# Causal mask added by VectorE inside the search for the row maximum, in place of a bf16 product on TensorE

## The chip, the cores and the metric

The kernel runs on one core of one Trainium2 chip. Its time is the device time of that core in microseconds (us). The kernel before takes 991.48 us, the median of 3 runs from 991.26 to 991.74. Below, TensorE is PE (its weight loads are PEld), VectorE is DVE, ScalarE is ACT, GpSimd is POOL and SyncE is SP.

## The reference, cut to what matters

One layer of a hybrid encoder over 512 tokens of width 1024. The change touches its two causal mixers. Forgetting attention ("fox") has 8 heads of width 64 and works on blocks of 128 queries:

```
logits = einsum('bhqd,bhkd->bhqk', qi, kf) + ci[..., :, None] - c[..., None, :]
logits = jnp.where(kpos[None, :] <= qpos[:, None], logits, -jnp.inf)
p = jax.nn.softmax(logits, axis=-1)
```

The mLSTM ("ml", 4 heads of width 128) needs the same of a matrix of decay logarithms, which is masked with a lower triangle, and of which every row's maximum is taken before the exponential:

```
Dlog = jnp.where(tri, Dlog, -jnp.inf)
m_t = jnp.maximum(inter_log, jnp.max(Dlog, axis=-1))
Dw = jnp.exp(Dlog - m_t[..., None])
```

The rest of the layer (projections, causal convolution, gates, cross-attention over 256 memory rows, an MLP of width 4096, norms) is not touched.

## The kernel before, in words

All large weights are streamed in units (`UNITS`): a unit is a slab of 512 weight columns. SP loads them in lots of 1 MB into `stage`, ACT copies a pair of slabs to a rounded part `w_hi`, and DVE subtracts that from the original to give the rest, `w_lo`. A product is then three matmuls, high by high, high by low and low by high, all at line 1062 in `half`. A "half" is four slabs deep, so twelve matmuls of 512 columns.

`make_steps` writes one list of steps, and every engine runs the steps that concern it in the order of that list, with semaphores between engines. Softmax work is laid between the halves. The 16 fox tasks t (4 pairs of heads by 4 query blocks, `PAIRS` by `NT`) stand two halves apart: `pair_scores` t on PE, `pair_exp` and `pair_norm` on DVE and ACT behind it, `pair_turn` four halves later and `pair_values` six halves later. Task t has 128, 256, 384 or 512 keys as t runs through 0, 1, 2, 3 of each pair. The 16 ml tasks follow, one half apart. While the first half of the fox tasks run, the same DVE and ACT queues also do the causal convolution (lines 622, 685, 814, 863).

Fox scores (line 1126): for each of the two heads of a pair, four matmuls add up in a PSUM bank, bank 2 for the one head and bank 3 for the other. Each has 64 rows of the array, one head on rows 0 to 63, the other on rows 64 to 127, and the two run side by side. Then comes the mask (line 1128): for each head a matmul of the bf16 identity `ident_b` with `hide_b`, a 128x128 bf16 tile that holds -1e30 above the diagonal, added to the last 128 columns of the bank. The ml scores (lines 1170 to 1172) do the same in one bank of 2 and 3.

DVE then finds the maximum of each row: for fox one `tensor_reduce` over both banks, negated (line 929), for ml one over one bank (line 951). ACT takes the exponential with that maximum as its bias (lines 705, 719). ml also has an instruction that multiplies and sums in one (`tensor_tensor_reduce`, line 960).

The tiles that live through the kernel are allocated one behind another. All activations lie behind them, at offsets from `a0`, which is the end of the former (`nc.sbuf_base`). Before the change `a0` is 95360 bytes, which is 745 times 128.

Of the kernel before, what the change touches and what calls it, by code (L numbers as in the profile page):

```python
# [6 lines left out]
F32R = mybir.dt.float32r  # L7
BF16 = mybir.dt.bfloat16
I32 = mybir.dt.int32
# [4 lines left out]
P = 128  # L14
# [27 lines left out]
X0 = N_ML  # L42
KB = 1024


# [216 lines left out]
def trunk(nc, x, mem, norm_mix, norm_xattn, norm_mem, norm_mlp, w_in, b_fox_f, b_mlstm_i, b_mlstm_f,  # L262
# [6 lines left out]
    with ExitStack() as ctx:  # L269
# [3 lines left out]
        def sb(name, shape, dt=F32):  # L273
            return ctx.enter_context(nc.sbuf_tensor(name, shape, dt))
# [5 lines left out]
        ident = sb("ident", [P, P])  # L280
        ident_b = sb("ident_b", [P, P], BF16)
        hide_b = sb("hide_b", [P, P], BF16)
        rows = FOX_HEADS + ML_HEADS
# [28 lines left out]

        a0 = nc.sbuf_base

# [192 lines left out]
        def _(pool):  # L507
            n = 0

            def fill(ins):  # L510
                nonlocal n
                ins.then_inc(s_const, 1)
                n += 1

            fill(pool.memset(ones[:], 1.0))
            fill(pool.memset(ident[:], 0.0))
            fill(pool.memset(ident_b[:], 0.0))
            fill(pool.memset(hide_b[:], 0.0))
            fill(pool.memset(upto[:], 1.0))
# [6 lines left out]
            pool.wait_ge(s_const, n)  # L526
            for m in (ident, ident_b):
                fill(pool.affine_select(out=m[:], in_=m[:], compare_op=ALU.not_equal, fill=1.0, base=0,
                                        pattern=[[-1, P]], channel_multiplier=1))

            fill(pool.affine_select(out=hide_b[:], in_=hide_b[:], compare_op=ALU.is_ge, fill=HIDE, base=0,
                                    pattern=[[-1, P]], channel_multiplier=1))

# [49 lines left out]
        def _(act):  # L583
# [87 lines left out]
            for step, n in steps:  # L671
# [27 lines left out]
                elif step == "pair_exp":  # L699
                    keys = P * (n % NT + 1)  # L700
                    act.wait_ge(s_fpeak, n + 1)
                    if n >= 2:
                        act.wait_ge(s_fturn, n - 1)
                    for d in range(2):
                        act.activation((prob, prob_b)[n % 2][:, d, 0:keys], bank[2 + d][:, 0:keys], ACT.Exp,
                                       bias=peak[:, d:d + 1],
                                       accum_out=pair_total[:, n % 2, d:d + 1]).then_inc(s_fexp, 1)
                elif step == "pair_turned":
# [55 lines left out]
        def _(dve):  # L764
# [113 lines left out]
            for step, n in steps:  # L878
# [48 lines left out]
                elif step == "pair_exp":  # L927
                    dve.wait_ge(s_fscore, n + 1)
                    dve.tensor_reduce(peak[:], two[1][:, :, 0:P * (n % NT + 1)], AX_X, ALU.max, negate=True)\
                       .then_inc(s_fpeak, 1)  # L930
                elif step == "pair_norm":
# [15 lines left out]
                elif step == "probs":  # L947
                    h, i, keys = task(n)
                    i2, row = n % 2, FOX_HEADS + task(n)[0]
                    dve.wait_ge(s_score, n + 1)  # L950
                    link(dve.tensor_reduce(ml_m[:, i2, 0:1], bank[2 + i2][:, 0:keys], AX_X, ALU.max))

# [59 lines left out]
        def _(pe):  # L1012
# [98 lines left out]
            def pair_scores(t):  # L1111
                p, i = t // NT, t % NT
                keys, tok = P * (i + 1), slice(P * i, P * i + P)
                cols = slice(decay_at(i), decay_at(i) + keys)
                if t == 0:
                    pe.wait_ge(s_dlow, NT + 1)
                if i == 0:
                    taken(pe, GROUP0[UNIT["fox_k"]] + p)
                if t >= 1:
                    pe.wait_ge(s_fexp, 2 * t)  # L1120
                for q in range(4):
                    for d in range(2):
                        r = slice(FOX_HD * d, FOX_HD * d + FOX_HD)
                        still = pick[r, 2 * p + d:2 * p + d + 1].to_broadcast([FOX_HD, P]) if q == 3 else (fq_hi, fq_hi, fq_lo)[q][r, p, tok]
                        moving = decay[r, cols] if q == 3 else (fk_hi, fk_lo, fk_hi)[q][r, p, 0:keys]
                        pe.matmul(bank[2 + d][:, 0:keys], still, moving, start=(q == 0), stop=False)  # L1126
                for d in range(2):
                    ins = pe.matmul(bank[2 + d][:, P * i:keys], ident_b[:], hide_b[:], start=False, stop=True)
                ins.then_inc(s_fscore, 1)
# [28 lines left out]
            def scores(t):  # L1158
                h, i, keys = task(t)
                s = bank[2 + t % 2]  # L1160
                cols = slice(decay_at(i), decay_at(i) + keys)
                if t == 0:
                    pe.wait_ge(s_silu, KT)
                    pe.wait_ge(s_fpt, N_FOX)
                    pe.wait_ge(s_fexp, 2 * N_FOX)
                else:
                    pe.wait_ge(s_prob, t)
                if t >= 2:
                    pe.wait_ge(s_exp, t - 1)
                pe.matmul(bank[5][:, 0:keys], ml_q[:, h, P * i:P * i + P], ml_k[:, h, 0:keys], start=True, stop=True)  # L1170
                pe.matmul(s[:, 0:keys], pick[0:64, FOX_HEADS + h:FOX_HEADS + h + 1].to_broadcast([64, P]), decay[0:64, cols], start=True, stop=False)
                pe.matmul(s[:, P * i:keys], ident_b[:], hide_b[:], start=False, stop=True).then_inc(s_score, 1)

# [104 lines left out]
N_SMALL = 6  # L1278
N_CONST = 21

# [24 lines left out]
```

## Time and profile before

| | |
|---|---|
| time, median of 3 runs | 991.48 us (991.26 to 991.74) |
| the profiled execution's own time | 991.38 us |
| its span, first to last instruction | 989.6 us |
| mean granted TensorE clock | 0.995 |
| PE busy | 958.0 us, 97% of the span |
| DVE busy | 478.6 us, 48% |
| ACT busy | 349.6 us, 35% |
| POOL busy | 13.7 us, 1% |

The span leaves out 1.78 us before the first and behind the last instruction. Durations of matmuls are from entry to modelled end, and matmuls are pipelined: two that follow each other begin 0.23 us apart though each is given 0.39 us. What PE spends on one is read from the distance of starts. The share of busy time of DVE and ACT is an average over stages; in a stage where they and PE wait for each other in turn, a lower share can still set the pace.

### The profile page before, as it was taken

The page shows a single profiled execution, that of the slowest core. Times are in us where ns is not written, and L with a number is a line of the kernel's source. Part 1 is how long each engine was busy: PE and PEld are TensorE (multiplying, and loading weights), DVE is VectorE, ACT ScalarE, POOL GpSimd, SP SyncE. Part 2 cuts the span into 40 slices and gives each one's busy share as a digit, 9 for nine tenths or more (in the row PEclk, how much of TensorE's full clock was granted, in tenths as well). Part 3 has the DMA queues.
Part 4 walks back from the last instruction along what each step waited for, and adds up shares of the span by engine and source line. Part 5 has one row for each costly group of instructions (what it writes and reads, how often), then busy time and mean ns, then how long its engine had stood idle before and what let it go on. Part 6 is the DMA issues. An engine that isn't in the chain of part 4 may idle for free.

```text
span 989.6 us, 11656 instructions
## 1 busy us (share of the span) xinstructions
PE 958.0 (97%) x4681; PEld 776.8 (78%) x4681; DVE 478.6 (48%) x873; ACT 349.6 (35%) x562; POOL 13.7 (1%) x37
## 2 busy tenths in 40 slices
PE   7999999999998999999999999999999999999996
PEld 6778777777776788889877668888888888888885
DVE  5622666433557654677234435643344434334536
ACT  4431555434324323235244422442144123213411
POOL 4000000000000000000000000000000000000000
PEclk9999999999999999999999999999999999999999
DMA  8212221122112162333422222222223332222212
GB/s 280 94 37 83 86 86 43 44 85 85 45 42 86 43 255 85 107 128 113 164 85 85 86 85 85 86 85 85 85 86 99 126 117 86 85 85 85 88 41 85
DMA packets 44205, 92.60 MB, mean 94 GB/s; under 512 B 1676, under 2 KB 1768, under 8 KB 44152
## 3 DMA queue, kind: packets, MB, share of 16 engines
q1 hardware_dynamic: 42584, 86.54, 26.2%
q0 software_dynamic: 1568, 5.32, 1.7%
q8 instruction: 37, 0.61, 0.2%
q14 instruction: 16, 0.13, 0.0%
HBM read 89.76 MB, written 2.10 MB: 93 GB/s over the span
## 4 chain that ended last, share of the span: by engine, by line
PE 86%; DVE 8%; ACT 3%; issue 1%; DMA 1%; SPq 0%; ACTq 0%; DVEq 0%
PE bank L1062 75%; DVE w_lo L794 3%; PE bank L1232 1%; DVE conv_acc L814 1%; PE bank L1075 1%; PE bank L1183 1%; PE bank L1126 1%; PE bank L1170 1%; ACT w_hi L585 1%; DMA stage<-in_w_in 1%; PE bank L1153 1%; PE bank L1197 1%; PE bank L1138 1%; PE bank L1210 1%; PE bank L1086 1%
## 5 line engine op out<-in xcount | busy, mean ns | idle before, releaser
L1062 PE MATMUL bank<-act_hi,w_hi 128*128 128x512 f32 (+2 forms) x624 | 246.2, 395 | 2.4 <-DVE act_lo L890 2.4
L1062 PE MATMUL bank<-act_hi,w_lo 128*128 128x512 f32 (+2 forms) x624 | 241.1, 386 | 0.0
L1062 PE MATMUL bank<-act_lo,w_hi 128*128 128x512 f32 (+2 forms) x624 | 240.9, 386 | 0.0
L794 DVE TENSOR_TENSOR w_lo<-stage,w_hi 128x1024 fp32r<-128x1024 f32 x156 | 183.9, 1220 | 112.6 <-ACT w_hi L585 112.4
L585 ACT ACTIVATE w_hi<-stage 128x1024 fp32r<-128x1024 f32 x156 | 156.4, 1051 | 187.1 <-PE bank L1062 179.8
L1062 PE MATMUL bank<-w_hi,act_hi 128*128 128x512 f32 x448 | 176.8, 395 | 5.1 <-DVE act_lo L890 3.5
L1062 PE MATMUL bank<-w_lo,act_hi 128*128 128x512 f32 x448 | 175.1, 391 | 0.0
L1062 PE MATMUL bank<-w_hi,act_lo 128*128 128x512 f32 x448 | 175.0, 391 | 0.0
L1062 PEld LDWEIGHTS bank<-act_hi,w_hi 128*128 128x128 f32 x624 | 117.8, 189 | 24.7 <-issue 2.6
L1062 PEld LDWEIGHTS bank<-act_hi,w_lo 128*128 128x128 f32 x624 | 117.7, 189 | 23.8
L1062 PEld LDWEIGHTS bank<-act_lo,w_hi 128*128 128x128 f32 x624 | 117.9, 189 | 22.0
L1062 PEld LDWEIGHTS bank<-w_hi,act_hi 128*128 128x128 f32 x448 | 84.4, 188 | 23.6 <-DVE act_lo L890 4.0
L1062 PEld LDWEIGHTS bank<-w_hi,act_lo 128*128 128x128 f32 x448 | 84.5, 189 | 17.7
L1062 PEld LDWEIGHTS bank<-w_lo,act_hi 128*128 128x128 f32 x448 | 84.6, 189 | 17.2 <-issue 0.2
L847 DVE TENSOR_TENSOR h_tok<-bank,h_tok 128x512 f32<-128x512 f32 x48 | 33.1, 689 | 92.5 <-PE bank L1062 91.8
L853 DVE TENSOR_TENSOR relu<-relu 128x512 f32<-128x512 f32 x32 | 22.1, 690 | 64.8 <-ACT relu L646 64.8
L646 ACT ACTIVATE relu<-bank 128x512 f32<-128x512 f32 x32 | 19.2, 599 | 77.9 <-PE bank L1062 77.9
L856 DVE TENSOR_TENSOR act_lo<-relu,act_hi 128x512 fp32r<-128x512 f32 x32 | 22.2, 693 | 22.4 <-ACT act_hi L585 22.4
L585 ACT ACTIVATE act_hi<-bank 128x512 fp32r<-128x512 f32 x32 | 17.7, 596 | 37.2 <-PE bank L1075 30.0
L585 ACT ACTIVATE act_hi<-relu 128x512 fp32r<-128x512 f32 x32 | 20.2, 633 | 24.8 <-DVE relu L853 24.8
L814 DVE SCALAR_TENSOR_TENSOR conv_acc<-conv_u,param,conv_acc 128x512 f32<-128x512 f32 x24 | 18.1, 752 | 19.0 <-ACT conv_acc L622 18.4
L719 ACT ACTIVATE dwt<-bank,ml_m 128x128 f32<-128x128 f32 (+3 forms) x16 | 8.4, 528 | 45.2 <-DVE ml_m L955 45.2
(220 smaller groups left out, 919.3 us busy)
## 6 DMA issues: line engine op xcount, KB each, us to landing
stage<-in_w_in SPq DMA_DIRECT2D x22, 1024.0 KB, 5.1
stage<-in_w_mlp_in SPq DMA_DIRECT2D x16, 1024.0 KB, 5.3
stage<-in_w_mlp_out SPq DMA_DIRECT2D x16, 1024.0 KB, 5.1
stage<-in_w_xkv SPq DMA_DIRECT2D x8, 1024.0 KB, 5.0
stage<-in_w_mix_out SPq DMA_DIRECT2D x4, 1024.0 KB, 5.1
stage<-in_w_xq SPq DMA_DIRECT2D x4, 1024.0 KB, 5.2
stage<-in_w_xo SPq DMA_DIRECT2D x4, 1024.0 KB, 5.2
x_tok<-in_x SPq DMA_DIRECT2D x4, 512.0 KB, 11.8
```

Of the source, the lines that this page charges most:

```text
L585: return act.activation(dst, src, ACT.Copy, **k)
L646: act.activation(relu[:, a % 2, :], b[:], ACT.Relu).then_inc(free, 1)
L794: dve.tensor_tensor(w_lo[:, r:r + 2, :], src, w_hi[:, r:r + 2, :].bitcast(F32), ALU.subtract)\
L814: ins = dve.scalar_tensor_tensor(acc, u[:, q:q + TOK], conv_taps[:, c, q:q + 1], acc, ALU.mult, ALU.add)
L847: dve.tensor_tensor(dst, b[:], dst, ALU.add).then_inc(free, 1)
L853: dve.tensor_tensor(relu2[:, a % 2, :], relu[:, a % 2, :], relu[:, a % 2, :], ALU.mult)\
L856: dve.tensor_tensor(act2_lo[:, a % KT, :], relu2[:, a % 2, :], act2_hi[:, a % KT, :].bitcast(F32), ALU.subtract).then_inc(s_al, 1)
L1062: ins = pe.matmul(dst, still[q], moving[q], start=(k == 0 and q == 0), stop=(k == nk - 1 and q == 2))
L1075: ins = pe.transpose(bank[2 + 2 * (n % 2) + b][:, P * q:P * q + P], scaled[:, n % 2, P * k:P * k + P], ident[:])
L1086: ins = pe.matmul(bank[6][0:16, :], w[:, k, :], a[:, k, :], start=(k == 0 and q == 0), stop=(k == KT - 1 and q == 2))
L1126: pe.matmul(bank[2 + d][:, 0:keys], still, moving, start=(q == 0), stop=False)
L1138: ins = pe.transpose(bank[4 + d][:, P * j:P * j + P], (prob, prob_b)[t % 2][:, d, P * j:P * j + P], ident[:])
```

## The change

The two bf16 tiles go, and a tile `hide` comes: 128 partitions by 512 f32, 0 in the first 384 columns, and in the last 128 columns -1e30 above the diagonal. Its last `keys` columns are the mask of a task with that many keys. The mask matmuls at lines 1128 and 1172 go. In place of each maximum by `tensor_reduce`, DVE runs a `tensor_tensor_reduce` that reads the bank and `hide`, adds them, writes the sum back to the bank and keeps the maximum. For fox this is one instruction a head instead of one for both, and what it writes is the negated sum, with a minimum kept; ACT's exponential takes it with a scale of -1. `s_fpeak` counts two a task instead of one. POOL fills one tile less and runs one `affine_select` less. `a0` is rounded up to a multiple of 128 bytes: it comes out at 96896 bytes, 757 times 128, and `nc.sbuf_base` is that number too.

```diff
-        ident_b = sb("ident_b", [P, P], BF16)
-        hide_b = sb("hide_b", [P, P], BF16)
+        hide = sb("hide", [P, TOK])
...
-        a0 = nc.sbuf_base
+        a0 = -(-nc.sbuf_base // ALIGN) * ALIGN
...
-            fill(pool.memset(ident_b[:], 0.0))
-            fill(pool.memset(hide_b[:], 0.0))
+            fill(pool.memset(hide[:], 0.0))
...
+            fill(pool.affine_select(out=hide[:, TOK - P:TOK], in_=hide[:, TOK - P:TOK], compare_op=ALU.is_ge, fill=HIDE,
+                                    base=0, pattern=[[-1, P]], channel_multiplier=1))
...
                 elif step == "pair_exp":
                     keys = P * (n % NT + 1)
-                    act.wait_ge(s_fpeak, n + 1)
+                    act.wait_ge(s_fpeak, 2 * (n + 1))
...
-                        act.activation((prob, prob_b)[n % 2][:, d, 0:keys], bank[2 + d][:, 0:keys], ACT.Exp,
-                                       bias=peak[:, d:d + 1],
-                                       accum_out=pair_total[:, n % 2, d:d + 1]).then_inc(s_fexp, 1)
+                        act.activation((prob, prob_b)[n % 2][:, d, 0:keys], bank[2 + d][:, 0:keys], ACT.Exp, scale=-1.0,
+                                       bias=peak[:, d:d + 1], accum_out=pair_total[:, n % 2, d:d + 1]).then_inc(s_fexp, 1)
...
                 elif step == "pair_exp":
                     dve.wait_ge(s_fscore, n + 1)
-                    dve.tensor_reduce(peak[:], two[1][:, :, 0:P * (n % NT + 1)], AX_X, ALU.max, negate=True)\
-                       .then_inc(s_fpeak, 1)
+                    keys = P * (n % NT + 1)
+                    for d in range(2):
+                        logits = bank[2 + d][:, 0:keys]
+                        dve.tensor_tensor_reduce(logits, logits, hide[:, TOK - keys:TOK], -1.0, -HIDE, ALU.add, ALU.min,
+                                                 peak[:, d:d + 1]).then_inc(s_fpeak, 1)
...
-                    link(dve.tensor_reduce(ml_m[:, i2, 0:1], bank[2 + i2][:, 0:keys], AX_X, ALU.max))
+                    s = bank[2 + i2][:, 0:keys]
+                    link(dve.tensor_tensor_reduce(s, s, hide[:, TOK - keys:TOK], 1.0, HIDE, ALU.add, ALU.max,
+                                                  ml_m[:, i2, 0:1]))
...
-                        pe.matmul(bank[2 + d][:, 0:keys], still, moving, start=(q == 0), stop=False)
-                for d in range(2):
-                    ins = pe.matmul(bank[2 + d][:, P * i:keys], ident_b[:], hide_b[:], start=False, stop=True)
+                        ins = pe.matmul(bank[2 + d][:, 0:keys], still, moving, start=(q == 0), stop=(q == 3))
...
-                pe.matmul(s[:, 0:keys], pick[0:64, FOX_HEADS + h:FOX_HEADS + h + 1].to_broadcast([64, P]), decay[0:64, cols], start=True, stop=False)
-                pe.matmul(s[:, P * i:keys], ident_b[:], hide_b[:], start=False, stop=True).then_inc(s_score, 1)
+                pe.matmul(s[:, 0:keys], pick[0:64, FOX_HEADS + h:FOX_HEADS + h + 1].to_broadcast([64, P]), decay[0:64, cols], start=True, stop=True)\
+                  .then_inc(s_score, 1)
...
-N_CONST = 21
+N_CONST = 19
```

No step changes its place in the list. What stands in DVE's row around the second and third fox task (t = 1 and 2), before:

```order
83 L929 TENSOR_REDUCE peak<-bank 128x2 [waits s_fscore]
84 L814 SCALAR_TENSOR_TENSOR conv_acc<-conv_u,param,conv_acc 128x512 [waits s_taken0]
85 L814 SCALAR_TENSOR_TENSOR conv_acc<-conv_u,param,conv_acc 128x512 [waits s_chain] x2
86 L934 RECIPROCAL inv<-pair_total 128x2 [waits s_fexp]
87 L937 TENSOR_SCALAR prob_b<-prob_b,inv 128x256 [waits s_chain]
88 L937 TENSOR_SCALAR prob_b<-prob_b,inv 128x256
89 L929 TENSOR_REDUCE peak<-bank 128x2 [waits s_fscore]
90 L863 SCALAR_TENSOR_TENSOR ml_q<-conv_th,conv_acc 128x512 [waits s_tanh]
```

and after (lines stand a few lower, since lines above are gone):

```order
86 L928 ISA bank,peak<-bank,hide 128x256 [waits s_fscore]
87 L928 ISA peak 128x1
88 L928 ISA bank,peak<-bank,hide 128x256
89 L928 ISA peak 128x1
90 L810 SCALAR_TENSOR_TENSOR conv_acc<-conv_u,param,conv_acc 128x512 [waits s_taken0]
91 L810 SCALAR_TENSOR_TENSOR conv_acc<-conv_u,param,conv_acc 128x512 [waits s_chain] x2
92 L933 RECIPROCAL inv<-pair_total 128x2 [waits s_fexp]
93 L936 TENSOR_SCALAR prob_b<-prob_b,inv 128x256 [waits s_chain]
94 L936 TENSOR_SCALAR prob_b<-prob_b,inv 128x256
95 L928 ISA bank,peak<-bank,hide 128x384 [waits s_fscore]
```

One instruction became two, each with a read-out of its accumulator behind it; the neighbours are the same.

## Rows read from the trace of the kernel before

**Rows 1.** The page: busy us, share of the span, instructions; granted clock in 40 slices.

```profile
PE 958.0 (97%) x4681; PEld 776.8 (78%) x4681; DVE 478.6 (48%) x873; ACT 349.6 (35%) x562; POOL 13.7 (1%) x37
PEclk9999999999999999999999999999999999999999
```

**Rows 2.** PE's waits, 150:200 us: who waited for whom, us, times, longest.

```profile
PE bank L1153 <- ACT prob_t L585: 2.3, 2, 1.8
```

**Rows 3.** The chain that ended last, 129:181 us: start us, us, what.

```profile
133.63 0.34 DVE peak L929
...
177.25 0.61 DVE peak L929
...
179.87 1.09 PE bank L1153 x16
```

**Rows 4.** Timeline of PE, 219.4:223 us: start us, us, engine, line.

```profile
219.45 0.39 PE L1062 MATMUL bank<-act_hi,w_lo 128*128 128x512 f32 x1
219.77 0.44 PE L1153 MATMUL bank<-prob_t,fox_v 128*64 128x128 f32 x4
...
221.29 0.40 PE L1126 MATMUL bank<-fk_hi,fq_lo 64*128 64x512 f32 x2
221.53 0.39 PE L1126 MATMUL bank<-decay,pick 64*128 64x512 f32 x2
221.85 0.29 PE L1128 MATMUL bank<-hide_b,ident_b 128*128 128x128 bf16 x2
221.95 0.48 PE L1062 MATMUL bank<-act_hi,w_hi 128*128 128x512 f32 x1
222.26 0.40 PE L1062 MATMUL bank<-act_lo,w_hi 128*128 128x512 f32 x1
```

**Rows 5.** Timeline of PE, 243.1:244.2 us.

```profile
243.24 0.32 PE L1171 MATMUL bank<-decay,pick 64*128 64x128 f32 x1
243.50 0.23 PE L1172 MATMUL bank<-hide_b,ident_b 128*128 128x128 bf16 x1
...
243.85 0.39 PE L1062 MATMUL bank<-act_lo,w_hi 128*128 128x512 f32 x1
```

**Rows 6.** Timeline of PE, 65.1:66.5 us.

```profile
65.93 0.50 PE L1062 MATMUL bank<-act_hi,w_hi 128*128 128x512 f32 x1
...
66.27 0.39 PE L1062 MATMUL bank<-act_lo,w_hi 128*128 128x512 f32 x1
```

**Rows 7.** Lines 929, 951: ns of one, least/median/most, first and last start, forms.

```profile
L929 DVE TENSOR_REDUCE peak<-bank x16: 417/820/1225, 104.7 to 222.2; 128x2 f32<-128x256 f32 x4, 128x2 f32<-128x512 f32 x4, 128x2 f32<-128x768 f32 x4, 128x2 f32<-128x1024 f32 x4
...
L951 DVE TENSOR_REDUCE ml_m<-bank x16: 283/487/691, 243.8 to 317.1; 128x1 f32<-128x128 f32 x4, 128x1 f32<-128x256 f32 x4, 128x1 f32<-128x384 f32 x4, 128x1 f32<-128x512 f32 x4
```

**Rows 8.** Timeline, 292:297 us.

```profile
293.76 0.49 PE L1171 MATMUL bank<-decay,pick 64*128 64x512 f32 x1
294.18 0.23 PE L1172 MATMUL bank<-hide_b,ident_b 128*128 128x128 bf16 x1
...
294.45 0.69 DVE L951 TENSOR_REDUCE ml_m<-bank 128x1 f32<-128x512 f32 x1 [2.85 <-PE bank L1172]
...
296.34 0.69 DVE L960 CUSTOM_DVE_ANT_0 prob<-bank,dwt 128x512 f32<-128x512 f32 x1 [0.76 <-ACT dwt L719]
...
296.96 0.08 DVE L960 DVE_READ_ACCUMULATOR2_ANT ml_den<- 128x1 f32 x1
296.96 0.68 DVE L995 SCALAR_TENSOR_TENSOR ml_h<-ml_th,bank 128x512 f32<-128x512 f32 x1
```

**Rows 9.** Timeline, 301.5:304.5 us.

```profile
302.58 0.28 DVE L951 TENSOR_REDUCE ml_m<-bank 128x1 f32<-128x128 f32 x1
...
304.24 0.52 PE L1197 MATMUL bank<-ident,prob 128*128 128x128 f32 x3 [1.82 <-ACT prob_t L585]
```

**Rows 10.** Timeline, 0:20 us.

```profile
6.90 0.19 POOL L544 CAST pick<-pick_row 128x12 fp32r<-128x12 f32 x1
...
8.79 1.09 PE L1075 MATMUL bank<-ident,scaled 128*128 128x128 f32 x8 [0.49 <-DVE scaled L874]
```

More of the change, by code:

```diff
@@ L7 @@
 F32R = mybir.dt.float32r
-BF16 = mybir.dt.bfloat16
 I32 = mybir.dt.int32
@@ L43 @@
 KB = 1024
+ALIGN = 128
 def make_units():
@@ L526, in _ @@
             pool.wait_ge(s_const, n)
[L527 to L531, printed above, removed]
+            fill(pool.affine_select(out=ident[:], in_=ident[:], compare_op=ALU.not_equal, fill=1.0, base=0,
                                     pattern=[[-1, P]], channel_multiplier=1))
+            fill(pool.affine_select(out=hide[:, TOK - P:TOK], in_=hide[:, TOK - P:TOK], compare_op=ALU.is_ge, fill=HIDE,
+                                    base=0, pattern=[[-1, P]], channel_multiplier=1))
             fill(pool.affine_select(out=upto[:], in_=upto[:], compare_op=ALU.is_ge, fill=0.0, base=0,
```

## The prediction, made before the changed kernel ran

> **What bounds the kernel now.** I read the page first: PE is busy for 97% of the span, DVE for 48% and ACT for 35%, with the clock at the upper level (2.4 GHz) all through [rows 1]. So what PE spends counts nearly everywhere, and what DVE spends counts only where PE waits for it. PE's waits come next. Between 150 and 200 us line 1153, which multiplies probabilities with values, waits twice for ACT's `prob_t`, 2.3 us in all [rows 2]. The chain that ended last shows why. From 129 to 180 us it does not run through PE but through DVE and ACT in turn, since convolution, splitting of weights and softmax share their two queues there. The search for the maximum, DVE line 929, is on that chain for six tasks in a row, t = 4 to 9, the first at 133.63 us, the last at 177.25 us. The chain comes back to PE at 179.87 us [rows 3]. So one and the same edit meets two situations: fox tasks 0 to 3 and 10 to 15, and nearly all of ml, where PE sets the time; and six fox tasks where DVE does.
>
> **What leaves PE.** 32 fox mask products and 16 ml ones go. The trace prices a pair of fox ones not by their length but by the distance of starts. The mask starts at 221.85, the first large matmul behind it at 221.95, the second at 222.26: 0.41 us from the start of the mask to the second large matmul [rows 4]. Without the mask the first large matmul would start where the mask does, and not sooner. Changing from the 64-row pieces of the scores to the full array has PE wait: the last score pair starts at 221.53 and the next at 221.85, 0.32 us later, where two of one shape stand 0.24 us apart (221.29 and 221.53). The step from full to half-width pieces costs the same 0.32 us, and there the type is f32 on both sides (219.45 to 219.77) [rows 4]. So I take it that the geometry makes the gap and not bf16, and that the large matmul inherits it. What does a large matmul then need until its successor starts? After small transposes that do not fill the array it is 0.34 us (65.93 to 66.27) [rows 6]. So a fox task saves 0.41 - 0.34 = 0.07 us. For an ml task it is 0.35 us from mask to second large matmul (243.50 to 243.85) [rows 5], so it saves 0.01 us. The mask product was almost wholly laid in the shadow of the large matmul's restart.
>
> A page of the Trainium skill prices it higher: "TensorE: Matmul & The Clock Gate", section "Back-to-back issue gap", has a matmul of 128 columns cost 128/2.4 + 2.5 = 56 ns, so 48 of them 2.7 us. Fox's two are at 0.10 us here (221.85 to 221.95), which agrees, but the ml one is not (rows 5), and the page says nothing of the restart behind, which the rows say is paid either way. By that rule the result would be the second rival below.
>
> **What comes to DVE.** The trace has no instruction of DVE that writes to PSUM. The nearest is line 960, the same kind of instruction, which reads a bank and a tile and writes a tile: 0.69 us for 512 columns, and what stands behind it (line 995) starts 0.62 us after it, at 296.96, in the same moment as the read-out of the accumulator, 0.08 us [rows 8]. A fox task with 512 keys would take 0.62 + 0.69 = 1.31 us for two, against 1.22 us for the one reduction (1225 ns) [rows 7]: +0.09 us. The fixed part of an instruction is paid twice, and that is alike for all four sizes. Lower end: 0, if the second hides wholly behind the first, and I see no reason for a gain, since as many elements are read. If both read-outs stand in line, 2 x (0.62 + 0.08) = 1.40 us, +0.18 us. The upper end is an instruction that takes the add and the maximum one after the other; one pass over 512 columns is 0.69 us (691 ns) [rows 7], so +0.69 us an instruction, for 128 columns +0.28. I take +0.09, which is what the row nearest in kind gives. For ml it is one for one, 0.69 against 0.69 us [rows 8], +0.01 with the read-out.
>
> A rule of the skill speaks against the split: "VectorE: DVE Perf Modes", section on the TRN2 errata, says that a fixed latency is exposed between instructions and charges an operation from PSUM 120 cycles at 0.96 GHz, 0.125 us, on top of its elements. By it a second instruction a task costs 0.125 us, where lines 960 and 929 give 0.09; over six tasks that is 0.2 us more than my sum.
>
> **Where each counts.** Fox tasks 0 to 3 and 10 to 15 are on PE's account: 10 x 0.07 = 0.70 us gained. DVE's 0.09 us is hidden there by the four halves of matmuls between scores and `pair_turn`; when that cover is gone it costs 0.09 a task, as next. For tasks 4 to 9 PE's gain is lost, since it only waits longer for `prob_t` at line 1153, and DVE's extra is on the chain: 6 x 0.09 = 0.54 us lost. Nor does it help that the scores are done sooner there, since DVE comes to them late; behind the new instructions on DVE wait the SiLU of the convolution (line 863) and the next `conv_acc`, and ACT waits for both. For ml, 14 of 16 tasks stand directly ahead of large matmuls: 14 x 0.01 = 0.14 us gained. At 294 us DVE waits for PE's mask: it ends at 294.18 + 0.23 = 294.41, the decay product ahead of it at 293.76 + 0.49 = 294.25 [rows 8]. DVE starts 0.16 us sooner and spends 0.01 more, and this leads on to PE's wait of 1.82 us for `prob_t` at 304.24 [rows 9]: 0.15 us gained.
>
> Edits at nothing: POOL's tiles are ready at 7.09 us, and the first transpose, which waits for them, starts at 8.79 because of `scaled` [rows 10]; one fill more or less there is covered by 1.7 us. ACT's scale is an operand that it has anyway. `s_fpeak` still makes the first exponential wait for what before was one instruction. The alignment changes no number: the former start was a multiple of 128 bytes, so is the new one, both are 128 over a multiple of 512, and all behind the mask tiles moves by 1536 bytes.
>
> Sum: -0.70 + 0.54 - 0.14 - 0.15 = -0.45 us. The profiled execution took 991.38 us (span 989.6 and 1.78 around it), which gives 990.9; the median of the runs is 0.10 above it, 991.48, which gives **991.0 us**. A measurement of this kernel tells apart about 0.2%, 2.0 us. So: no change that can be told.
>
> **Rivals.** First, slower: a DVE instruction that reads and writes the same bank gets through one column in two cycles and not one. For: no row has it, and nothing in the trace writes PSUM besides PE. Against: line 960 reads two sources and writes at one column a cycle. Each instruction then takes one more pass, 0.28, 0.41, 0.55 or 0.69 us by keys (rows 7, the two between by the slope of the ends). On the chain that is for t = 4 to 9 (1, 2, 3, 4, 1, 2 blocks of keys) 0.56 + 0.82 + 1.10 + 1.38 + 0.56 + 0.82 = 5.2 us, and for ml at 294 and 302.58 [rows 9] 0.69 + 0.28 = 1.0 us: 991.0 + 6.2 = 997.2 us. It decides as slower once a fox task on the chain loses over (2.0 + 0.45) / 6 = 0.4 us more than I put down.
>
> Second, each mask product costs its full time and no restart is left behind: 0.10 us a fox task and, taken at half of that, 0.05 an ml task give 10 x 0.10 + 14 x 0.05 = 1.7 us in place of my 0.84, so 990.1 us. For: the 0.10 between 221.85 and 221.95. Against: 0.31 behind it.
>
> Third, faster: the gap between score pieces and the next was made by the change of type to bf16, and now the large weights load ahead under the last score product. Then its successors stand 0.23 us apart at once: 0.73 us (221.53 to 222.26) becomes 0.46, and for ml 0.61 (243.24 to 243.85) becomes about 0.34. That is 10 x 0.27 + 14 x 0.27 = 6.5 us in place of 0.84: 985.3 us. For: the products on both sides are of one kind now. Against: the gap from 219.45 to 219.77, with no bf16 near.
>
> That the change does not do what it says I don't count: 48 products are gone from PE's row and 32 + 16 new instructions stand in DVE's.
>
> **How the numbers follow.** Forecast 0.71, first rival 0.12, second 0.10, third 0.07. The time is the forecast's. Around it: the longer read-out adds 0.5 us, and a first rival that bites for half adds 3.1 us, which makes the upper end 991.0 + 0.5 + 3.1 = 994.6. The lower takes in the second rival with DVE's extra at 0 (990.1 - 0.5 = 989.6) and the scatter of 0.2: 989.4. What is left out is the full first rival and the third, 0.19. Faster by over 0.2% (under 989.5): the third rival and 0.03 of the others, 0.10. Slower (over 993.5): the first and 0.04 of the forecast's edge, 0.16. Within: 0.74.
>
> **What would show it.** In the profile after, the two new instructions of a task with 512 keys should last 1.31 us together, those of one with 256 or more the same +0.09; 0.69 each with 1.38 or more would be the first rival. From the last decay product to the second large matmul it should be 0.32 + 0.34 = 0.66 us, where 0.46 would be the third rival. The chain should still pass through DVE from 129 to 180 us, with line 1153 released about 0.25 us later than now (0.54 lost, 4 x 0.07 gained before), and PE's wait ahead of it longer by as much and by what PE saved. The forecast is wrong if another wait of PE appears between 180 and 240 us, or if the convolution's chain is moved past a point where it collides with a load of weights.

## The result, and the profile after

| | before | after |
|---|---|---|
| median of 9 runs each (lowest to highest), us | 991.48 (989.91 to 993.01) | 994.5 (992.9 to 996.55) |
| ratio, 95% interval | | 1.0027 (1.0018 to 1.0036) |
| profiled execution, us | 991.38 | 994.5 |
| its span, us; mean granted clock | 989.6; 0.995 | 992.8; 0.991 |

The changed kernel is 3.0 us slower by the medians and 2.7 by the ratio, just past the 0.2% that a measurement can tell. The forecast, 0.45 us faster and so "no change", was wrong. That the time is still inside the range, at its upper end, is luck: 3.1 us of that end stood for a first rival that bites for half, and nothing of it came; other losses filled its place. The page after reads as follows (busy us, share of the span, instructions).

```profile
PE 959.3 (97%) x4633; PEld 777.8 (78%) x4633; DVE 482.2 (49%) x937; ACT 349.8 (35%) x562; POOL 13.6 (1%) x35
```

PE has 48 instructions fewer than in [rows 1], DVE 64 more, and yet PE's busy time went up by 1.3 us. Fewer products and more busy time point to a lower clock somewhere, which the row of tenths on the page does not show.

**Where the 3.2 us of span are.** I laid the starts of the same PE instructions of both traces beside each other. After minus before, in us:

| at (us of before) | 131 | 180 | 244 | 293 | 304 | 560 | 629 | after 637 | end |
|---|---|---|---|---|---|---|---|---|---|
| later by | -0.40 | +1.57 | +1.04 | +1.10 | +1.07 | +1.29 | +1.31 | +2.86 | +3.2 |

There are three parts: a loss of 2 us from 130 to 180 us, a small gain up to 244 us, and a jump of 1.5 us at 629 us, in the MLP, 300 us behind the last instruction that the change touches. Besides these, 0.2 us are added at 305 to 320 us and 0.3 us at the very end: +2.86 still holds at 980 us and behind it, and the last DVE instruction starts 0.27 us late behind an idle engine, at 988.32 us (+3.10). Why it does is open.

**The first part: DVE and ACT.** The chain that ended last in the changed kernel, 104 to 136 us and then 175 to 183 us (start us, us, what):

```profile
103.68 1.13 DVE w_lo L790
104.81 0.21 DVE bank L928
...
110.24 0.34 DVE bank L928
...
116.33 0.47 DVE bank L928
...
123.29 0.61 DVE bank L928
...
130.66 1.05 ACT w_hi L582
131.74 2.36 DVE w_lo L790 x2
134.10 0.21 DVE bank L928
```

```profile
178.63 0.34 DVE bank L928
...
180.47 0.92 ACT prob_t L582
181.44 1.09 PE bank L1152 x16
```

It now goes through DVE and ACT without a break from 101.36 us on, where ACT copies a pair of slabs; the stretch above opens in the middle of the subtraction behind that. The fox tasks t = 0 to 3 (104.81, 110.24, 116.33, 123.29) stand on it too, which I had put on PE's account. Against [rows 3] the task at 133.63 starts at 134.10, 0.47 us later, although PE was 0.40 us ahead by then. The one at 177.25 starts at 178.63, +1.38, and the values at 179.87 start at 181.44, +1.57. PE's waits between 100 and 150 us (who waited for whom, us, times, longest) show that what PE saved there it only waited:

```profile
PE bank L1152 <- ACT prob_t L582: 2.5, 2, 2.0
```

Before, the same row read 1.2 us, once.

What one task costs is seen in t = 7, both heads with 512 keys. Timeline of DVE, before and then after (start us, us, engine, line, operation):

```profile
157.13 1.22 DVE L929 TENSOR_REDUCE peak<-bank 128x2 f32<-128x1024 f32 x1
158.27 0.68 DVE L863 SCALAR_TENSOR_TENSOR ml_k<-conv_th,conv_acc 128x512 f32<-128x512 f32 x1
```

```profile
158.16 0.69 DVE L928 CUSTOM_DVE_ANT_0 bank<-bank,hide 128x512 f32<-128x512 f32 x1
158.77 0.14 DVE L928 DVE_READ_ACCUMULATOR2_ANT peak<- 128x1 f32 x1
158.77 0.73 DVE L928 CUSTOM_DVE_ANT_0 bank<-bank,hide 128x512 f32<-128x512 f32 x1
159.42 0.14 DVE L928 DVE_READ_ACCUMULATOR2_ANT peak<- 128x1 f32 x1
159.42 0.69 DVE L859 SCALAR_TENSOR_TENSOR ml_k<-conv_th,conv_acc 128x512 f32<-128x512 f32 x1
```

The second peak is there 1.40 us after the start (159.42 + 0.14 - 158.16), where it was 1.22: +0.18. That is exactly the end that I had worked out with both read-outs in line, and had not taken. The instruction behind it on DVE starts 1.26 us after, where it was 1.14: +0.12. The instruction itself takes 0.69 us for 512 columns, so the first rival (two cycles a column, 1.38 us) fell at once. From the start of t = 4 to that of the values six tasks add 1.10 us, 0.18 each. The four ahead of them add 0.18 each too, 0.72 in all, and 0.47 is left of it because DVE had some slack at t = 3: there it still waited 0.15 us for PE's scores in the kernel before, and PE is ahead now.

```profile
122.91 1.22 DVE L929 TENSOR_REDUCE peak<-bank 128x2 f32<-128x1024 f32 x1 [0.15 <-PE bank L1128]
```

**The second part: PE.** Timeline of PE after, around the last fox task:

```profile
222.69 0.39 PE L1127 MATMUL bank<-decay,pick 64*128 64x512 f32 x2
223.01 0.50 PE L1063 MATMUL bank<-act_hi,w_hi 128*128 128x512 f32 x1
...
223.35 0.40 PE L1063 MATMUL bank<-act_lo,w_hi 128*128 128x512 f32 x1
```

The gap of geometry is there without any bf16 (222.69 to 223.01, 0.32 us) and the restart behind it is 0.34 (223.01 to 223.35): 0.66 us, as predicted, where [rows 4] have 0.73. Of the third rival nothing came. From 180 to 244 us six fox tasks give back 0.53 us, 0.09 each, a little over my 0.07, since more than the last products moved. In ml, from 244 to 293 us, nothing is gained: the step from the decay product to the second large matmul is 0.59 us (244.30, 244.55, 244.89) where [rows 5] have 0.61, but the two kernels go from 1.04 to 1.10 us apart.

**The third part: the clock.** Windows of 8 us, columns: stretch, length, busy us of PE, PEld, DVE, ACT and POOL with their instructions, granted clock, share of the DMA engines, GB/s. Before, then after:

```profile
304.00:312.00 8.00, 7.76 (x38) 5.85 (x39) 6.39 (x25) 3.52 (x6) 0.00 (x0) 1.00 0.35 128
629.00:637.00 8.00, 7.98 (x49) 7.96 (x50) 6.15 (x15) 3.36 (x6) 0.00 (x0) 1.00 0.45 132
```

```profile
304.00:312.00 8.00, 6.69 (x27) 5.30 (x28) 5.99 (x27) 4.18 (x7) 0.00 (x0) 0.79 0.37 131
629.00:637.00 8.00, 6.67 (x29) 6.70 (x30) 7.09 (x16) 3.04 (x4) 0.00 (x0) 0.79 0.41 133
```

In the changed kernel the clock falls to its lower level (1.2 GHz) for part of both windows, in the kernel before in neither. At 629 us PE comes out of a wait of 2.4 us for `act_lo` in both kernels. The timeline of PE there, before and after:

```profile
629.02 0.41 PE L1062 MATMUL bank<-act_hi,w_hi 128*128 128x384 f32 x1 [2.40 <-DVE act_lo L890]
...
629.62 0.34 PE L1062 MATMUL bank<-act_hi,w_hi 128*128 128x384 f32 x1
629.80 0.35 PE L1062 MATMUL bank<-act_lo,w_hi 128*128 128x384 f32 x1
```

```profile
630.34 0.41 PE L1063 MATMUL bank<-act_hi,w_hi 128*128 128x384 f32 x1 [2.43 <-DVE act_lo L886]
...
631.40 0.52 PE L1063 MATMUL bank<-act_lo,w_hi 128*128 128x384 f32 x1
631.72 0.52 PE L1063 MATMUL bank<-act_hi,w_lo 128*128 128x384 f32 x1
```

The wait is as long as before and only 1.31 us later in the program's time, but behind it the same products stand 0.32 us apart and not 0.18, for 3.4 us. That costs 1.55 us. The fall at 305 us costs little, some 0.2 us, because DVE sets the pace from 304 to 315 us. A third such stretch, at 91 us behind the small products of the forget gates, is in both profiles, and so are one at 13 to 17 us and one behind the last products, at the end.

### The profile page after: what moved, and what is told of

Its sections match the earlier page's. It is cut to its first block, busy times and chain, and to the rows that moved or that the text cites. A ratio compares the mean times of both kernels' runs of the same rounds, so it can differ in the third digit from the quotient of the medians.

```text
span 992.8 us, 11621 instructions
## 1 busy us (share of the span) xinstructions
PE 959.3 (97%) x4633; PEld 777.8 (78%) x4633; DVE 482.2 (49%) x937; ACT 349.8 (35%) x562; POOL 13.6 (1%) x35
## 4 chain that ended last, share of the span: by engine, by line
PE 83%; DVE 9%; ACT 4%; issue 1%; DMA 1%; SPq 0%; ACTq 0%; DVEq 0%
PE bank L1063 74%; DVE w_lo L790 3%; DVE conv_acc L810 2%; PE bank L1231 1%; ACT w_hi L582 1%; PE bank L1076 1%; PE bank L1182 1%; PE bank L1169 1%; PE bank L1209 1%; DMA stage<-in_w_in 1%; DVE bank L928 1%; PE bank L1196 1%; PE bank L1152 1%; ACT prob_t L582 1%; PE bank L1137 1%
```

## The experiments

Ratios are to the runs of the kernel before on the same chip (24 to 35 runs each, medians 991.75, 991.8 and 991.2 in the three groups). Two marks help in comparing profiles: "values" is the start of line 1152/1153 at about 180 us; whether the clock fell at 91 us varies from one execution to the next and moves all behind it by 1.5 us, so values are compared among profiles of one kind. Without that fall the level of before is 178.31 us (from the kernel `tail`, below, which is as before up to there), with it 179.87.

**fox_only and ml_only: each half alone.** The first takes the fox part of the change and leaves ml as it was, the second the reverse.

```diff
 # fox_only: ml as before
-                    link(dve.tensor_tensor_reduce(s, s, hide[:, TOK - keys:TOK], 1.0, HIDE, ALU.add, ALU.max,
-                                                  ml_m[:, i2, 0:1]))
+                    link(dve.tensor_reduce(ml_m[:, i2, 0:1], bank[2 + i2][:, 0:keys], AX_X, ALU.max))
```

> The kernel after with the ml tasks as before (bf16 mask on PE, tensor_reduce on DVE); fox masked by DVE. Theory A (the loss is DVE's: the pair of instructions of a fox task lasts 0.18 us longer than the one reduction, for the ten tasks t = 0 to 9 whose DVE and ACT work is one unbroken chain): line 1152 is released at about 181.4 us as in the kernel after, and the time is 1.0 to 1.5 us over before, more where the clock dips. Rival B (the loss comes from the ml tasks or from behind 300 us): the time is that of before within 0.5 us.

> The kernel after with the fox tasks as before; only ml is masked by DVE. Theory A: chain of DVE and ACT up to 180 us as before (line 1153 released at 179.9), ml costs at most 0.07 us a task where DVE is on the path, two or three tasks: time of before within 0.5 us. Rival B: 1 to 3 us slower, with a lower clock around 305 or 630 us.

fox_only: 994.08 us, 1.0018 (1.0009 to 1.0028). ml_only: 991.45 us, 1.0002 (0.9988 to 1.0015). The loss is in the fox half. In fox_only's profile the clock does not fall at 91 us and the values start at 179.93, 1.6 us behind the level of its kind; it falls at 305 and at 629 us. In ml_only the values start at 179.82 and it falls at neither.

**no_mask and both_masks: the price of PE's part.** no_mask is the kernel before with the mask left out, both_masks the changed kernel with PE's mask products put back, so that the mask is added twice.

```diff
 # no_mask
-                for d in range(2):
-                    ins = pe.matmul(bank[2 + d][:, P * i:keys], ident_b[:], hide_b[:], start=False, stop=True)
```

> The kernel before without any mask product: fox and ml attend to later tokens of their block too. What PE gains alone. Theory A: a fox task takes 0.10 us less of PE, but from 104 to 180 us DVE and ACT set the pace, so that gain is lost for t = 0 to 9, and the six tasks behind give 0.6 us, ml about 0.2: 0.8 us faster than before. Rival C (the forecast's account, PE gains for t = 0 to 3 too): 1.1 us. Rival D (the large weights load ahead once no bf16 product stands between): 6 us faster.

> The kernel after with the bf16 mask products on PE as well, so the mask is added twice. What DVE costs alone. Theory A: DVE's chain ends 1.57 us later at 180 us, plus 0.1 to 0.2 for ml: 1.7 us slower than before, plus 1.5 where the clock dips behind a wait. Rival B: no slower than before, if the loss came from the geometry of PE's row.

no_mask: 991.6 us, 1.0 (0.9988 to 1.0013). All 48 products together are worth nothing that the runs can tell, though the interval leaves room for 1.2 us. In its profile, which ran beside before's with the same clock, PE is 0.56 us ahead at 223 us and 1.16 at 320 us, and this stays to the end; at the values it is ahead by 0.07 only (179.80 against 179.87). The ml part of this, 0.6 us, is more than the 0.2 expected: 0.60 ahead at 244 us, 0.68 at 293, 0.84 at 304, 1.16 at 320. So what PE saves in the first ten fox tasks goes into its waits. both_masks: 995.59 us, 1.0032 (1.0021 to 1.0044), by the ratios 0.5 us above the changed kernel. The clock falls at 305 and 629 us there as well, and in this execution at 148 us too.

**split_reduce and tile_out: what in DVE's part costs.** split_reduce is the kernel before with one reduction for each head; tile_out is the changed kernel with the fox sums written to the probability tile in SBUF, where ACT then reads them, and not back to PSUM.

```diff
 # split_reduce
-                    dve.tensor_reduce(peak[:], two[1][:, :, 0:P * (n % NT + 1)], AX_X, ALU.max, negate=True)
+                    for d in range(2):
+                        dve.tensor_reduce(peak[:, d:d + 1], bank[2 + d][:, 0:P * (n % NT + 1)], AX_X, ALU.max, negate=True)
 # tile_out
-                        dve.tensor_tensor_reduce(logits, logits, hide[:, TOK - keys:TOK], ...)
+                        dve.tensor_tensor_reduce((prob, prob_b)[n % 2][:, d, 0:keys], bank[2 + d][:, 0:keys], hide[:, TOK - keys:TOK], ...)
```

> The kernel before, with one tensor_reduce for each head in place of one for both; PE keeps the mask. It splits the 0.18 us that a fox task costs DVE. Theory A (half is the second fixed part, half the accumulator read-out behind the second): a task costs 0.07 to 0.08 us more than before, and line 1153 is released 0.7 us later at 180 us. Rival (all of it is the read-outs): no change; rival (all of it the split): 1.6 us later.

> The kernel after, with the negated sums of fox written to the tile of the probabilities in SBUF and not back to the bank; ACT reads them there. Theory A (the read-out behind a write to PSUM is 0.14 us where behind a write to SBUF it is 0.08): 0.06 us less a fox task on DVE, less the difference that ACT has between reading SBUF and PSUM, some 0.04 us twice a task, so about nothing in time. Rival (writing to PSUM is what costs): the fox pair lasts as long as the reduction before, 1.22 us at 512 keys, and the time returns to that of before.

Timeline of DVE in split_reduce and then in tile_out, the same task t = 7:

```profile
155.90 1.28 DVE L930 TENSOR_REDUCE peak<-bank 128x1 f32<-128x512 f32 x2
```

```profile
158.01 0.69 DVE L929 CUSTOM_DVE_ANT_0 prob_b<-bank,hide 128x512 f32<-128x512 f32 x1
158.62 0.09 DVE L929 DVE_READ_ACCUMULATOR2_ANT peak<- 128x1 f32 x1
158.62 0.69 DVE L929 CUSTOM_DVE_ANT_0 prob_b<-bank,hide 128x512 f32<-128x512 f32 x1
159.23 0.09 DVE L929 DVE_READ_ACCUMULATOR2_ANT peak<- 128x1 f32 x1
```

The split alone makes 1.22 into 1.28 us, +0.06; with the read-outs it is 1.31 where the sum goes to SBUF (159.23 + 0.09 - 158.01) and 1.40 where it goes to PSUM. So of 0.18 us a task 0.06 is the split, 0.03 the read-out as it is behind SBUF (1.31 - 1.28), and 0.09, the half, is what writing to PSUM adds: 0.05 on the last read-out and 0.04 on the second instruction (0.73 against 0.69). Over ten tasks split_reduce moves the values by 0.53 us (178.84, no fall at 91 us), tile_out by 1.34 (181.21, with it): it saves on DVE, but ACT's exponential reads SBUF 0.03 to 0.04 us slower than PSUM (medians of the odd and the even tasks 608 and 503 ns, in the changed kernel 577 and 468), two of them a task. In time: 992.44 us, 1.0011 (1.0001 to 1.0021), and 992.49 us, 1.0012 (1.0001 to 1.0023). split_reduce's runs are barely told from before's, and its profile too has the falls at 305 and 629 us.

**tail: the change where PE sets the time.** DVE adds the mask for fox tasks t = 10 to 15 only; t = 0 to 9 and ml stay as before.

```diff
+BY_DVE = 10
+                    if n < BY_DVE:
+                        dve.tensor_reduce(peak[:], two[1][:, :, 0:keys], AX_X, ALU.max, negate=True)
```

> DVE masks only the fox tasks t = 10 to 15, which lie where PE sets the pace; t = 0 to 9 and ml keep the mask product and their reductions. Theory A: 6 x 0.10 = 0.6 us faster than before, nothing lost before 180 us; that is under what a measurement can tell. Rival (the loss is not bound to where DVE is on the path): half a microsecond or more slower.

991.12 us, 0.9994 (0.9984 to 1.0004); its lowest run is 989.35, those of before in the three groups 989.74, 989.83 and 989.56. The loss is gone, as the theory of DVE's chain has it. The gain of the six tasks is below what the runs can tell, but the profile has it: against before PE is 1.56 us ahead at the values, since the clock does not fall at 91 us here, 2.02 at 223 us and 2.03 at 980: 0.46 us for six tasks.

**after_warm and before_warm: the clock at 629 us.** Ten products of the identity with itself, into a bank that nothing reads, are put on PE in the wait at 629 us.

```diff
+                    if n == FIRST_HALF[UNIT["mlp_in0"]]:
+                        for _ in range(KEEP_WARM):
+                            pe.matmul(bank[7][:, 0:P], ident[:], ident[:], start=True, stop=True)
```

> The kernel after, with ten 128x128 matmuls of the identity on PE in the 2.4 us in which it waits for act_lo ahead of the first MLP unit (629 us); their result goes to a bank that nobody reads. Theory A (of the 3.0 us, 1.5 come from the clock, which fell to half behind this wait in the profile after and not in that of before): no lower clock behind 629 us, runs fall into steps 1.6 us apart and the median is 1 to 1.6 us under that of the kernel after. Rival (the clock has nothing to do with that wait): the median stays at 994.5.

> The kernel before, with the ten idle matmuls of after_warm at 629 us. Theory A (in the kernel before the clock falls behind that wait in some executions only, in the kernel after in every one): the median falls by 0 to 1.6 us, less than the 1.7 us it fell for the kernel after, and the slowest step of its runs, 993.1, goes. Rival (it falls as often in both): the median falls by 1.6 us, to 990.

after_warm: 992.8 us, 1.0009 (1.0 to 1.0019), by the ratios 1.8 us under the changed kernel. Its two windows, columns as above:

```profile
304.00:312.00 8.00, 8.00 (x32) 5.75 (x30) 6.44 (x24) 2.99 (x5) 0.00 (x0) 0.79 0.32 122
629.00:637.00 8.00, 8.00 (x51) 7.96 (x50) 6.17 (x16) 3.15 (x6) 0.00 (x0) 1.00 0.46 139
```

The clock is at its upper level at 629 us and in the first window as low as in the changed kernel. Laid beside that kernel's profile, the same PE instructions are 1.6 us earlier from 100 to 629 us (no fall at 91 us) and 3.2 us earlier from 638 us to the end. before_warm: 991.36 us, 1.0003 (0.9989 to 1.0017). The same filler gives the kernel before nothing that the runs can tell, as it should if that kernel does not lose the clock there; in one profile of each it does not. The interval leaves room for 1.1 us, and one of the eleven runs, 992.88, is still on the slowest step.

**shift: a later arrival alone.** Is it the new instructions, or only that PE comes to the wait later? The kernel before, with the first pair of score products of t = 15 made three times more (0.7 us of PE at 221 us, discarded by `start`), has none of the change.

```diff
-                for q in range(4):
+                for q in (-3, -2, -1, 0, 1, 2, 3) if t == N_FOX - 1 else range(4):
```

> The kernel before, with the first pair of score products of the fox task t = 15 made three times more (0.7 us of PE, at 221 us; DVE and ACT have no more work). It asks what makes the clock fall at 305 and 629 us. Theory P (where these waits fall in time decides): the clock falls at both as in all six kernels whose work up to 180 us ends 0.7 to 2 us later, and the time is 0.7 + 1.5 = about 2.2 us over before. Theory W (a longer wait of PE decides): no fall there in the profile, 0.7 us over before.

```profile
304.00:312.00 8.00, 7.07 (x35) 5.27 (x36) 5.97 (x25) 4.18 (x7) 0.00 (x0) 1.00 0.38 133
629.00:637.00 8.00, 7.13 (x32) 7.16 (x33) 6.62 (x16) 3.04 (x4) 0.00 (x0) 0.79 0.40 131
```

993.68 us, 1.0027 (1.0016 to 1.0039), from 0.7 us of added work: the median is 2.5 us above before's in its group. PE starts behind the wait at 629.87 us (before: 629.02), and the clock falls at 630.99, but not at 305 us. So 0.7 us more of PE's products are enough for the fall at 629 us, and nothing of DVE's is needed for it. All six runs bear it out: the lowest, 992.14, is 2.6 us above before's lowest. That half of the expectation which named 305 us failed.

But no moment of the program's time decides. The first product behind the wait, in ml_only, fox_only and split_reduce:

```profile
628.93 0.41 PE L1069 MATMUL bank<-act_hi,w_hi 128*128 128x384 f32 x1 [2.41 <-DVE act_lo L895]
628.95 0.49 PE L1070 MATMUL bank<-act_hi,w_hi 128*128 128x384 f32 x1 [2.43 <-DVE act_lo L895]
628.50 0.41 PE L1063 MATMUL bank<-act_hi,w_hi 128*128 128x384 f32 x1 [2.41 <-DVE act_lo L890]
```

From 629 to 637 us the granted clock is 1.00 in ml_only and 0.79 in the other two, though one of these arrives with it and one 0.4 us earlier. Among executions of one kind, though, it is the later ones that lose it. Where the clock fell at 91 us too, no_mask (627.90), ml_only (628.93) and before (629.02) keep the clock, and shift (629.87), tile_out (630.18) and the changed kernel (630.34) lose it. Where it did not, tail (627.03) keeps it, and split_reduce and fox_only, 1.5 and 1.9 us later, lose it.

**off_64: the second half of the change.** The changed kernel with the activations 64 bytes further on.

```diff
-        a0 = -(-nc.sbuf_base // ALIGN) * ALIGN
+        a0 = -(-nc.sbuf_base // ALIGN) * ALIGN + 64
```

> The kernel after, with all activations 64 bytes further on, so that they start at a half of 128 bytes. It asks what the other half of the change, the multiple of 128 bytes, guards against. Theory A (the start address does not matter to any engine at this granularity): 994.5 us, all durations as in the kernel after. Rival (it does): matmuls at line 1063 or DVE's and ACT's passes last longer, and the kernel is slower by a per cent or more.

1008.25 us, 1.0174 (1.016 to 1.0188): by the ratios 1.5% above the changed kernel, by the medians 1.4%. The rival holds, and Theory A falls. Two groups of large matmuls by shape in off_64 and then in the changed kernel (count | busy us, mean ns | idle before). Behind the arrow stand the moving operand and then the stationary one:

```profile
L1063 PE MATMUL bank<-act_lo,w_hi 128*128 128x512 f32 x592 | 233.3, 394 | 0.0
...
L1063 PE MATMUL bank<-w_lo,act_hi 128*128 128x512 f32 x448 | 178.1, 397 | 0.0
```

```profile
L1063 PE MATMUL bank<-act_lo,w_hi 128*128 128x512 f32 x592 | 231.7, 391 | 0.0
...
L1063 PE MATMUL bank<-w_lo,act_hi 128*128 128x512 f32 x448 | 174.9, 390 | 0.0
```

By distance of starts a matmul whose stationary operand is an activation takes 233.3 ns in place of 227.0, one whose moving operand is one 230.2 in place of 227.5. There are three groups of 448 of the first kind and three of 592 of the second: 1344 x 6.3 ns + 1776 x 2.7 ns = 13.3 us, of 13.6 us that the span grew. In the pair compared here both kernels start on a multiple of 128 bytes, so this half of the change neither gives nor takes; it keeps the next edit of the tiles ahead from costing 1.4%.

**tail_best: what the runs pointed to.** tail, with the filler at 629 us, and with the forget gates' running sums made by 5 products of 12 to 48 columns where there were 14 of 12 columns (each in two passes), so that the thin stretch ahead of 91 us takes 1.1 us and not 3.1.

```diff
-                for i in range(NT):
-                    pe.matmul(bank[6][:, rows * i:rows * i + rows], upto[:], forget[:, i, :], start=True, stop=True)
-                for i in range(NT):
-                    for u in range(i + 1):
-                        ...
+                pe.matmul(bank[6][:, 0:rows * NT], upto[:], forget[:].rearrange("p i g -> p (i g)"), start=True, stop=True)
+                for s in range(NT):
+                    ins = pe.matmul(bank[6][:, 64 + rows * s:64 + rows * NT], (ones if s else upto)[:],
+                                    forget[:, 0:NT - s, :].rearrange("p i g -> p (i g)"), start=(s == 0), stop=(s == NT - 1))
```

> tail (DVE masks t = 10 to 15 only) with the ten idle matmuls at 629 us, and with the sums of the forget gates at 88 to 91 us in five products in place of fourteen: one over the 48 columns of all four tiles where there were four of 12, and the cross-tile sums likewise. Theory A: 0.6 us from tail, 2 us from the nine products that go (0.22 us each at lines 1103 and 1106), and the clock no longer falls at 91 and 629 us, 1.6 us each where it did: median near 987.5, the runs closer together. Rival: the clock still falls at 91 us behind the narrow products of the decay rows: 989.

```profile
87.97 0.42 PE L1116 MATMUL bank<-forget,upto 128*128 128x48 f32 x2
88.22 0.39 PE L1119 MATMUL bank<-forget,upto 128*128 128x48 f32 x2
88.45 0.80 PE L1119 MATMUL bank<-forget,ones 128*128 128x36 f32 x6
89.11 0.49 PE L1076 MATMUL bank<-act_hi,w_hi 128*128 128x512 f32 x1
```

987.47 us, 0.997 (0.996 to 0.998): 0.3% under before and, by the ratios, 0.6% under the changed kernel. The timeline of PE shows the sums from 87.97 to 89.11 us, where before they ran from 87.82 to 90.97; behind them the clock stays at its upper level, here and at 629 us. How much of the gain each of the three edits has was not run apart; the shorter sums account for 1.9 us by the profile (the first large matmul behind them starts at 89.11 and not at 90.97). The filler shows no gain there, for in tail the clock does not fall at 629 us either.

## Why the prediction was wrong, point by point

**Which tasks are DVE's.** This step failed. I took the chain of waits at its word: it enters DVE at 129 us, so six tasks were on DVE's account and four (t = 0 to 3) on PE's, where DVE's extra was to be hidden by the four halves of matmuls behind the scores. The chain view follows the last releaser at each step, and at 129 us that was a tie between PE's products and ACT's queue; ahead of the tie DVE and ACT had hardly more slack than behind it, 0.25 us in four tasks. The changed kernel's chain is on them from 101.36 us, and before t = 4 DVE is 0.47 us late and PE's lead of 0.40 us gone into a wait. In my sum 4 x 0.07 of gain becomes 0.47 of loss. no_mask shows the same from the other side: ten tasks of PE's gain come to 0.07 us at the values.

**What a task costs on DVE.** The term was mis-sized: 0.09 forecast, 0.18 measured, the upper end that I named beside it. I had taken the instruction behind an accumulator as starting with the read-out (it does), and forgot that ACT, which is next on the chain, needs the end of the last read-out; and behind a write to PSUM that read-out is 0.14 us, where [rows 8] have 0.08. With 0.18 the six tasks cost 1.10 us and not 0.54.

**The rule on DVE's fixed latency.** The Trainium skill ("VectorE: DVE Perf Modes", the section on the TRN2 errata) makes, by its figure for an operation from PSUM, a second instruction cost 0.125 us a task. split_reduce, which has just that second instruction, shows 0.06 (1.28 against 1.22 us), so it is too high for the split by itself. The whole came to more than the rule because of the read-outs, of which it does not speak.

**What leaves PE.** Right in mechanism and nearly in size: 0.32 of geometry and 0.34 of restart, together 0.66 as predicted; 0.09 a fox task where I had 0.07. no_mask has PE's side of the ml terms alone: 0.08 us from 244 to 293 us where I had 0.14, and 0.16 from 293 to 304 us where I had 0.15. In the changed kernel neither is left. The 0.15 us at 294 us did not come: DVE does start sooner against PE (295.38 where [rows 8] have 294.45, +0.93 with PE's decay product at +1.10), but the read-out, 0.14 us long and waited for by the next instruction, brings it to +1.00, and the one at 303.79 us to +1.07 when PE is released. Two read-outs of 0.07 us net, on the path, took the gain. The price of 56 ns for 128 columns that the Trainium skill has in "TensorE: Matmul & The Clock Gate", section "Back-to-back issue gap", is its figure for a single isolated product; the same section says that in a stream with weight loads it is too low. Here it is near for fox (0.09 us a pair against 0.11) and too high for ml.

**The clock.** No step of mine had it: I read it as at its upper level all through from a row of tenths, though the windows show it at its lower level at 13 to 17, at 91 to 95 and from 986 us on in the kernel before, and the sum has no term for it. What has built up at 629 us is 1.31 us (1.57 at 180, less 0.53, and 0.27 more behind that, most of it with the clock's fall at 305 us). That alone would have been within 0.2%. Then the clock falls behind the wait of 2.4 us, which costs 1.55 us. after_warm takes this away and shift makes it without the change; before_warm, which finds nothing to take away, agrees with both. With 0.3 us at the very end the sum is the 3.2 us of the two profiles.

**What stays open.** Why the clock falls behind that wait in the kernels that come to it later, each within its kind of execution, and what decides at 305 us: shift did not bring that fall, tile_out and split_reduce did. What differs between executions with and without the fall at 91 us is not shown either. And whether the executions that were not profiled follow the same pattern; their times stand in steps of about 1.6 us (before: 989.7, 991.4, 993.1), which is what one fall costs, but the steps have no trace of their own.

## What to carry to other kernels

Where two queues such as DVE's and ACT's run without slack, an instruction that gets longer costs on every pass through them, also ahead of the point where the chain of waits first names them: lay their rows over the whole stretch and look for idle time, and count a lengthened instruction up to the moment its consumer is released, read-out included. Then look at the granted clock in narrow windows behind every wait of PE, in both kernels: 1.3 us of loss brought 1.5 us more 450 us later, and ten idle products in the wait took the second part back.

## What the runs showed of the hardware that I had not expected

- The read-out of DVE's accumulator took 0.142 us (139 to 144 ns, all 32) behind an instruction that wrote to PSUM, and 0.084 us (81 to 88 ns) behind one that wrote to SBUF; the instruction that started beside a read-out was 0.04 us longer in the first case.
- ACT's exponential of the same tile read SBUF 0.03 to 0.04 us slower than PSUM.
- Activations 64 bytes off a multiple of 128 cost each large matmul 6.3 ns as the stationary operand and 2.7 ns as the moving one, 1.4% in all.
- The clock fell behind a stretch of 3 us of 12-column products at 91 us in some executions, and behind a wait of 2.4 us in some kernels and not in others; the one at 629 us cost 1.55 us, and that at 91 us, by tail's profile, 1.56. No profile of before, ml_only, no_mask, tail or before_warm had it at 629 us; those of the changed kernel, fox_only, both_masks, split_reduce, tile_out, shift and off_64 all did.
